# Gate and up projection by seven quarter products in place of eight, with weight sums made in DRAM

## The reference

```python
h = h + jnp.concatenate([o_g, o_f], axis=-1) @ w_out[i]

hn = rmsnorm_2(h, ffn_norm_w[i])
gate, up = jnp.split(hn @ w_gate_up[i], 2, axis=-1)      # 1024 x 5632: 2816 gate and 2816 up columns
h = h + (jax.nn.silu(gate) * up) @ w_down[i]             # 2816 x 1024

ple_gate = jax.nn.sigmoid(rmsnorm_2(h, ple_norm_w[i]) @ w_ple_gate[i])
h = h + ple_gate * (p[i] @ w_ple_proj[i])
```

## Time and profile before

| what | before |
|---|---|
| median of 3 runs (lowest, highest) | 1207.83 us (1205.83, 1208.27) |
| span of the profiled execution | 1203.8 us |
| TensorE / VectorE / ScalarE / GpSimd busy | 98 / 58 / 42 / 5% |
| traffic | 118.21 MB, mean 98 GB/s |
| gate and up stage | about 786 to 1026 us |

### The profile page before, as it was taken

How to read it: one execution, slowest core, us unless ns; L and a number is a source line. 1 busy time by engine, 2 the same in 40 slices (tenths; PEclk the granted TensorE clock), 3 DMA queues, 4 the chain that set the end, 5 groups by cost and what they waited for, 6 DMA issues and landing times.

```text
span 1203.8 us, 15960 instructions
## 1 busy us (share of the span) xinstructions
PE 1181.7 (98%) x6570; PEld 959.3 (80%) x6570; DVE 702.3 (58%) x1074; ACT 501.1 (42%) x801; POOL 55.9 (5%) x54
## 2 busy tenths in 40 slices
PE   7999999999999999999999899999999999999997
PEld 5888778787777887877777888888888888888886
DVE  6776455556567765648886874554444444333355
ACT  5516524535634454224538444442322233222254
POOL 0190000000000100000000200000000000000000
PEclk9999999999999999999999999999999999999999
DMA  9762122122112533221212010222222322422321
GB/s 370 305 228 83 53 88 71 66 79 88 53 57 67 157 101 116 97 71 53 77 64 81 9 33 7 97 79 105 88 102 92 105 88 100 149 96 97 101 88 70
DMA packets 34136, 118.21 MB, mean 98 GB/s; under 512 B 3888, under 2 KB 4016, under 8 KB 34064
## 3 DMA queue, kind: packets, MB, share of 16 engines
q1 hardware_dynamic: 31824, 111.03, 26.4%
q0 software_dynamic: 1392, 4.72, 1.3%
q10 hardware_dynamic: 848, 1.45, 0.3%
HBM read 112.99 MB, written 4.19 MB: 97 GB/s over the span
## 4 chain that ended last, share of the span: by engine, by line
PE 93%; ACT 2%; DVE 2%; issue 1%; ACTq 0%; DVEq 0%
PE pb L651 90%; PE pb L914 1%; PE pb L742 1%; ACT Y L1374 1%; PE pb L1075 0%; DVE tmpf L1868 0%; ACT outT L1374 0%; ACT sp L1497 0%; DVE wlo L1868 0%; PE pb L1346 0%; ACT hhi L1374 0%; DVE Y L1868 0%; ACT sp L1499 0%; DVE sp L2032 0%; DVE fv L1868 0%
## 5 line engine op out<-in xcount | busy, mean ns | idle before, releaser
L651 PE MATMUL pb<-hhi,wlo 128*128 128x512 f32 (+2 forms) x1048 | 407.3, 389 | 2.6 <-DVE wlo L1868 2.6
L651 PE MATMUL pb<-hhi,whi 128*128 128x512 f32 (+2 forms) x1048 | 406.6, 388 | 0.0
L651 PE MATMUL pb<-hlo,whi 128*128 128x512 f32 (+2 forms) x1048 | 405.4, 393 | 0.6 <-DVE tmpf L1868 0.6
L1868 DVE TENSOR_TENSOR wlo<-raw,whi 128x1024 fp32r<-128x1024 f32 (+1 forms) x177 | 216.3, 1225 | 106.2 <-ACT whi L1374 105.4
L651 PEld LDWEIGHTS pb<-hhi,wlo 128*128 128x128 f32 (+1 forms) x1048 | 196.6, 188 | 44.5 <-DVE wlo L1868 3.5
L651 PEld LDWEIGHTS pb<-hlo,whi 128*128 128x128 f32 (+1 forms) x1048 | 196.4, 187 | 44.0 <-issue 3.5
L651 PEld LDWEIGHTS pb<-hhi,whi 128*128 128x128 f32 (+1 forms) x1048 | 196.4, 187 | 41.0
L1374 ACT ACTIVATE whi<-raw 128x1024 fp32r<-128x1024 f32 (+1 forms) x177 | 180.3, 1035 | 70.9 <-PE pb L651 49.7
L651 PE MATMUL pb<-alo,whi 128*128 128x512 f32 x176 | 68.5, 389 | 0.0
L651 PE MATMUL pb<-ahi,wlo 128*128 128x512 f32 x176 | 68.5, 389 | 0.0
L651 PE MATMUL pb<-ahi,whi 128*128 128x512 f32 x176 | 68.5, 389 | 0.0
(11 more groups left out here) (375 smaller groups left out, 1574.7 us busy)
## 6 DMA issues: line engine op xcount, KB each, us to landing
raw<-w_all SPq DMA_DIRECT2D x165, 512.0 KB, 3.5
adab<-ada_d SPq DMA_DIRECT2D x12, 512.0 KB, 12.6
gbt<-ada_d SPq DMA_DIRECT2D x12, 512.0 KB, 8.3
raw<-w_all SPq DMA_DIRECT2D x13, 384.0 KB, 3.0
xT<-xn_d SPq DMA_DIRECT2D x4, 512.0 KB, 12.8
ple_scratch<-zs SPq DMA_DIRECT2D x8, 256.0 KB, 5.7
xT<-x_d POOLq DMA_DIRECT2D x8, 256.0 KB, 3.0
out_d<-outT SPq DMA_DIRECT2D x3, 512.0 KB, 3.4
```

The costliest lines, as they stand in the source:

```text
L651: return e.matmul(out, lhs, rhs, start=start, stop=stop, skip_group_check=True)
L1868: return e.tensor_tensor(out, a, b, op)
```

## The change

Let the activations be cut into quarters: features 0 to 511 and 512 to 1023 (4 blocks of 128 each), tokens 0 to 255 and 256 to 511. The weights are cut into features x (gate, up). One level of Strassen's scheme makes the four output quarters (gate and up, early and late tokens) of seven products in place of eight, each of a sum of weight quarters and a sum of activation quarters. For every unit u (128 gate and 128 up columns, 22 of them) there are seven products of 4 blocks x 3 matmuls with 256 columns; PRODUCTS is their order, two products make a chunk ("st").

- **Weight sums.** Four of the seven left operands are sums of quarters. GpSimd makes them in DRAM: a copy w_sums<-w_all and accumulating transfers on top, 48 transfers in all (8 steps of five 128x2048 and one 128x1024), at most three in flight. 36 stand between the rope step and the eight xT loads, 12 behind the load of the masks. SyncE loads each chunk as two halves of 128x512.
- **Activation sums.** xhi and xlo hold seven quarters of each of 4 block pairs. Blocks 0 to 3 give quarters 0 and 1, blocks 4 to 7 with blocks 0 to 3 the other five, in the wo2 loop on ScalarE and VectorE.
- **Adding up.** Products 6 and 2 add into a copy of product 1 (seed, ScalarE, PSUM to PSUM), 3, 7 and 4 into sums with product 5, which ScalarE copies to SBUF (fifth, into bcst and a part of cst, no longer in use). VectorE makes third_seed, up_late, gate_early, gate_late and gated_up, half width each. Up is no longer scaled by 1/rms; the down projection's output is.
- **Space.** The activation pairs a take the room of the old tiles; units 0 to 3 are stored to DRAM (a_spill) and loaded back once the last product is done; the down projection takes them last (DOWN_K).
- Two pairs of semaphores become one each (rcf with posi, gcst with rmk), and the second four ple loads move from SyncE to GpSimd.

```diff
+LEFT = {1: ("sum", 0), 2: ("raw", 1), 3: ("sum", 1), 4: ("raw", 3), 5: ("raw", 2), 6: ("sum", 2), 7: ("sum", 3)}
+RIGHT = {1: 0, 5: 1, 7: 2, 2: 3, 3: 4, 4: 5, 6: 6}
+def products():
+    out = [(1, 0), (5, 0), (1, 1), (5, 1), (6, 0), (2, 0), (7, 0), (6, 1), (3, 0), (2, 1), (4, 0)]
+    for u in range(2, FFB):
+        out += [(1, u), (7, u - 1), (5, u), (3, u - 1), (6, u), (4, u - 1), (2, u)]
+    return out + [(7, FFB - 1), (3, FFB - 1), (4, FFB - 1)]
...
+            def sum_step(out, src, add):
+                for c in range(0, RUN, 2048):
+                    n = done[0]
+                    if n >= 3:
+                        G.wait_ge(*SUMS[n % 3](n - 3))
...
+                    if add:
+                        e.dma_start(o, i, accum_op=ALU.add).then_inc(SUMS[n % 3].sem, 16)
...
+            sum_step(sums[0], whole[0], False)
+            sum_step(sums[1], whole[0], False)
+            sum_step(sums[0], whole[1], True)
+            sum_step(sums[1], whole[2], True)
+            sum_step(sums[2], sums[0], False)
+            sum_step(sums[2], whole[2], True)
             for m in range(8):
                 G.wait_ge(*MG(m))
                 e.dma_start(xT[:, m, :], x_d[m * 128:m * 128 + 128, :]).then_inc(XBACK[m].sem, 16)
...
+            sum_step(sums[3], sums[2], False)
+            sum_step(sums[3], whole[3], True)
...
+            def product(p_, u):
+                hi, lo, w = weights_of("st", AT[p_, u] // 2)
+                k0, x = 4 * (AT[p_, u] % 2), RIGHT[p_]
+                b = FF_BANK[p_] + 4 * (u % 2)
+                T.wait_ge(*WLO(w))
+                if p_ in (1, 5):
+                    bank(b)
+                elif p_ in (6, 2):
+                    T.wait_ge(*FA(("seed", u)))
+                else:
+                    T.wait_ge(*FV_((("c22" if p_ == 4 else "c12"), u)))
+                for k in range(4):
+                    T.wait_ge(*LO(("w", k if x < 2 else k + 4)))
+                    t = mm3(PB[b][:, 0:256], hi[:, k0 + k, :], lo[:, k0 + k, :], xhi[:, k, x, :], xlo[:, k, x, :],
+                            k == 0 and p_ in (1, 5), k == 3)
...
+            for p_, u in PRODUCTS:
+                product(p_, u)
+                if (p_, u) == (5, 1):
                     T.wait_ge(*SS(("w", 7)))
                     sum_squares(7, "ffn", ssq[:, :])
+            for b in (4, 5):
+                free[b] = [FV_(("a", FFB - 1))]
...
+                V.wait_ge(*FA(("x", m)))
+                if m < 4:
+                    tt(x[:, m, 1, :], x[:, m, 0, :], x[:, m, 2, :], ALU.add).then_inc(FV_.sem, 1)
+                    if m:
                         squared("w", m - 1)
+                    low(("w", m), xlo[:, m, 0:2, :], x[:, m, 0:2, :], xhi[:, m, 0:2, :])
+                else:
+                    tt(y[:, 2:4, :], y[:, 0:2, :], x[:, k, 0:3:2, :], ALU.subtract)
+                    stt(y[:, 4, :], y[:, 0, :], -1.0, y[:, 1, :], ALU.mult, ALU.subtract)
+                    stt(y[:, 5, :], x[:, k, 0, :], -1.0, y[:, 1, :], ALU.mult, ALU.subtract).then_inc(FV_.sem, 1)
+                    squared("w", m - 1)
+                    low(("w", m), xlo[:, k, 2:7, :], y[:, 1:6, :], xhi[:, k, 2:7, :])
```

More of the change, by code:

```diff
@@ L55, in chunks @@
     out += [("wo2", i, 8, 128) for i in range(8)]
-    for j in range(FFB):
-        out += [("gt", j, 8, 128), ("up", j, 8, 128)]
+    out += [("st", i, 8, 128) for i in range(len(PRODUCTS) // 2)]
     for m in range(NB):
@@ L205, in build @@
         mod0 = sb(top, "mod0", [128, 24])
-        sb(top, "pad", [128, 4])
         xT = sb(top, "xT", [128, NB, S])
@@ L1790, in scalar_program @@
                     conv("wo2", *((m, LOOK + 1) if m > 4 else (min(m + 3, 5),)))
[L1791 to L1797 removed]
+                A.wait_ge(*TXR(("w", m)))
+                if m > 5:
+                    A.wait_ge(*LO(("w", m - 2)))
+                copy(xq4[:, m, 0:3:2, :] if m < 4 else xqs[:, m % 2, 0:2, :], xT[:, m, :].rearrange("p (a b) -> p a b", a=2),
+                     scale=vc(V_FN + m)).then_inc(FA.sem, 1)
@@ L1807, in scalar_program @@
+            silu(0)
+            conv_for(4, 0)
+            act_high(0)
+            for u in range(2, FFB):
+                conv_for(1, u)
+                seed(u)
+                conv_for(5, u)
+                fifth(u)
+                conv_for(3, u - 1)
+                silu(u - 1)
+                conv_for(4, u - 1)
+                act_high(u - 1)
+            conv("st", len(PRODUCTS) // 2 - 1)
+            silu(FFB - 1)
+            act_high(FFB - 1)
             for m in range(8):
@@ new lines, in vector_program @@
+            gated_up(0)
+            act_low(0)
+            for u in range(2, FFB):
+                conv_for(7, u - 1)
+                up_late(u - 1)
+                conv_for(3, u - 1)
+                gate_late(u - 1)
+                conv_for(6, u)
+                third_seed(u)
+                conv_for(4, u - 1)
+                gated_up(u - 1)
+                conv_for(2, u)
+                gate_early(u)
+                act_low(u - 1)
+            conv("st", len(PRODUCTS) // 2 - 1)
+            up_late(FFB - 1)
@@ L2647, in weights @@
         assert out[-1].size == 128 * kb * n, (name, i)
+    for half in range(2):
+        for k0 in (0, 4):
+            for u in range(FFB):
+                out.append(blocks_of(a["w_gate_up_2"][0], slice(128 * (FFB * half + u), 128 * (FFB * half + u + 1)), k0, 4))
     return np.concatenate(out)
```

279 lines of the change are left out of this document (200 added, 79 removed).

## The result

| what | before | after |
|---|---|---|
| median (lowest, highest), 20 runs each | 1207.39 us (1205.69, 1209.51) | 1211.32 us (1207.07, 1213.89) |
| span and run time of the profiled execution | 1203.8, 1205.6 us | 1211.5, 1213.27 us |
| mean granted clock of it | 0.998 | 0.989 |
| traffic | 118.21 MB | 185.97 MB |

The ratio is 1.0029, with an interval from 1.0021 to 1.0036: **slower by 0.3%**, where no change was forecast. The time lies inside the range. A run takes 1.8 us longer than its span in all runs of the changed kernel, so the trace shown of before is of one of its fastest executions (1205.6 us, worked out from its span) and that of after of one 1.95 us over its median: of the 7.7 us between the two spans, 3.9 are between the medians.

The account below looks back on a forecast made before the run. The changed stage was taken as bound by TensorE's step count times step length; 17.6 us saved less waits of 1.7, 10.4, 2.5 and 0.85 gains 2.15; with 0.7 clock and 1.0 contention, -0.45 us: 1207.4 us, range 1198 to 1236.

Parts of the forecast that it names:

- products: Gate and up stage: 1,056 matmuls at 0.2267 us become 1,848 at 0.120 us, 17.6 us less.
- wait for chunk 1: Start of the stage: TensorE waits 1.7 us for weight chunk 1, which VectorE converts just before block 6.
- wait for the sum of squares: Start of the stage: TensorE idles 10.4 us, until 804.2 us, while VectorE finishes block 7 and its square.
- sum to product (7,0): After the sum of squares: two products, then a 2.5 us wait for VectorE until 810.4 us; 0.7 us for the clock.
- bank 4 at the end: Stage end: the down projection waits 0.85 us after the last matmul for the last block's gated product.
- sums beside the weight loads: Weight loads delayed by the DRAM sum transfers: 1 us taken, bounds 0 and 10.
- serial chain: Activation preparation crossing between VectorE and ScalarE: 5.7 us per block from block 4, 6.85 with its weight chunk.
- shorter hole: Rival: start waits of 7.5 us in place of 14.6 and no clock loss, giving 1199.6 us; chance 0.27.
- 4.0 us more for what lies around the span: Median of the runs shown, 1207.83 us, against the profiled span of 1203.8 us; span differences were put on the median.
- Sums in DRAM: First 36 transfers: 200 us from 154.2 us, ending at 355, in time for xT; rival that they come late, chance 0.18.
- Starving: Rival: products wait for chunk loads once two 256 KB loads take over 5.1 us, giving 1222 us; chance 0.21.
- Reloads "nothing": Stage end: four reloads of spilled blocks take 10 us, wanted 12.2 us later, so no cost.

Follow-up runs that it names:

- e4: Changed kernel with useless matmuls in three TensorE waits (78 ahead of the sum of squares, 20 before and 5 behind product (4,21)); 1209.13 us, ratio 1.0017.
- e3: Changed kernel with the activation preparation interleaved: next block's residual ahead of this block's low part, next block's copy ahead of its weight chunk; 1198.01 us, ratio 0.9928.
- e2: e1 plus VectorE's two weight conversions for the down projection moved behind the last up_late and the last gate_late; 1205.85 us, ratio 0.9985.
- e1: Changed kernel with bank 4 freed once VectorE has read the last unit's early gate, not after the gated product; 1208.93 us, ratio 1.0019.
- e9: Kernel before the change, with useless matmuls (4 and 6) in TensorE's waits at 26.7 and 28.4 us; 1207.43 us, ratio 0.9997.
- e11: e8 plus three small edits: sum of squares behind product (6,0), ple loads after the spill reloads, waits at 27 and 28 us filled; 1189.65 us, ratio 0.9852.
- e8: Changed kernel with the edits of e2, e3, e5 and e6 together; 1191.00 us, ratio 0.9869.
- e5: Changed kernel with ScalarE making the high part of weight chunk 4 ahead of the logarithm, not behind its table load; 1206.66 us, ratio 0.9998.
- e10: e5 plus 13 useless matmuls (1.56 us) between products (2,0) and (7,0); 1210.09 us, ratio 1.0022.
- e6: Changed kernel with the last 12 weight-sum transfers moved right behind the first 36, ahead of the xT loads; 1209.09 us, ratio 1.0018.
- e7: Changed kernel without weight sums, every product taking a plain weight quarter, so the output is not the reference's; 1209.18 us, ratio 1.0015.

## Why the prediction was wrong

Measured against forecast, by the prediction's own steps, in the two traces:

| step | forecast | measured |
|---|---|---|
| products | -17.6 us | -17.5 (0.1201 us a step) |
| wait for chunk 1 | 1.7 | 1.64 |
| wait for the sum of squares | 10.4 | 9.76 |
| sum to product (7,0) | 6.2, and 0.7 for the clock | 7.58 (the sum alone 2.09, in e4 at full clock 1.14) |
| bank 4 at the end | 0.85 | 0.82 (e3, at full clock) |
| before (4,21) | none | **2.47** |
| clock at the end | none | **2.86** (e4) |
| sums beside the weight loads | 1.0 | 0.76 |
| low clock at 30 and 722 us | none | 1.4 + 1.6 in this trace |

- **The products** were right to a hundredth of a step, and so was the serial chain: 6.85 us for a block, measured 6.72; the sum of squares starts 0.5 us ahead of the forecast, once the 3.8 us by which the first residual was late are taken off. The rival "shorter hole" is out.
- **The term for the end of the stage is the step that failed.** "At the end bank 4 is free only when the last block's gated product is done, **0.85 us** after the last matmul" is all that the sum has there. The wait it names was there at its size, 0.82 us. The one before it, 2.47 us, was put at nothing without a reason, though the order shows it: between the last block's gate and its up_late VectorE has two weight conversions for the down projection. I had followed the queue behind each wait at the start of the stage, and not at its end. e2 shows it, with e1 beside it.
- **The clock** was weighed at the start only, and there my 0.7 us stands against 0.95 (e4: from sum to (7,0) 6.63 us without a fall, 7.58 with it). At the end, where the prediction has no term for it, 2.86 us came. e2 and e4 both remove the low clock. The two missing terms, 5.3 us, are more than the whole difference of the medians, 3.9 us: without them the change would have been faster than before by about 1.4 us (an estimate), near the forecast. That the time lies inside the range is owed to the range's width, which was drawn for other reasons: none of the rivals has a wait at the end.
- **"4.0 us more for what lies around the span"** was misread. It is 1.8 us. Of the other 2.2, 0.4 are that the median of three runs (1207.83 us) is above that of twenty (1207.39), and 1.8 that the profiled run is of the lowest group; the low clock at 720 us in the trace of e9 fits them.
- **Sums in DRAM.** 147 us for 36 transfers, I took 200; the last 12 disturb by 0.76 us in this trace, I took 1.0. Nine copies in a row were issued 3.6 us apart (161.64 to 190.51 us), nine accumulating transfers 5.5 (204.63 to 248.86). The Trainium skill (Collectives: The Full Stack, "The bandwidth ceiling") has half the rate for a reduction between cores because of the second source read; in the trace an accumulating transfer within one core has 0.65 of a copy's. The first 36 are through at 317 us, where my working by the rule gave 320.
- **Starving** did not occur: no wait for a load in the stage, at 192 GB/s.
- **Reloads "nothing"**: true in after, where the stage's end was late anyway; 0.6 us once it is not (e2, e11; 0.2 in e8).

The account of the two traces: -0.45 - 1.0 (the forecast's own term for the sums) + 3.75 (by so much the first residual is late: 1.4 and 1.6 for the low clock at 30 and 722 us, 0.76 for the transfers) + 0.2 (start hole) + 0.1 (steps) + 2.47 + 2.86 = 7.9 us; the spans differ by 7.7.

## What to carry to other kernels

- A scheme that saves matmuls moves the bound to the seams: look at what each engine has queued at the first and at the last product, at both ends with the same care. Here the inner part was right to 0.2 us, and 16.1 us of waits at the seams, with the low clock behind them, ate the 17.5 us saved; ordering the instructions anew gave 20 us back without removing one of them.
- A chain that crosses between two engines twice per block costs the sum of both. Put the next block's first step ahead of this block's last (e3: 6.72 to 5.0 us per block) before taking an engine to be the bound.
- Compare several runs before reading "what lies around the span" out of one trace, and take gains of under 3 us behind a wait of TensorE as unsafe: e5 and e10 differ by 1.56 us of useless work and by 3.4 us of time.

## What the runs showed of the hardware that I had not expected

- Whether a wait of about 2.5 us takes the clock down depends on more than its length. 2.47 us were followed by a fall in after, e1, e6, e7 and e10, and by none in e3 and e5; 1.53 us at 28 us, with 1.06 us just ahead of it, by one in after, e1, e3, e4, e8 and others, by none in before, e2 and e5. A low stretch lasted 3 to 10 us and cost up to 2.9. The Trainium skill (TensorE: Matmul & The Clock Gate, "Why this matters for your kernels") warns of the fall behind an idle gap; the runs agree (9.8 us ahead of the sum of squares), and add that the moment of the gap decides as well as its length (e5, e10).
- A wait filled with useless matmuls keeps the clock (e4), yet the next wait, longer by then, gets the fall.
- The sum of squares, two matmul records, takes 1.12 to 1.14 us at full clock (e3, e4, e8) and 2.09 at the lower one (after), all behind a wait of TensorE. With matmuls running right up to it, it takes 0.86 us at full clock (before).
- Three DRAM to DRAM transfers in flight at a time, at a mean queue share of 1.02 from 160 to 290 us (most of the first 36), slowed nothing there: TensorE's work from 163.04 to 297.73 us took 134.69 us, before 134.68.
